# Two attention heads per step instead of one, in the second block of a two-block transformer kernel

## What is computed

```python
def context_attention(q, k, v, sink=None):            # layer 0, context tokens
    s = jnp.einsum('bqhgd,bkhd->bhgqk', q, k)
    _, p = joint_softmax([sink_column(sink, s), s])
    o = jnp.einsum('bhgqk,bkhd->bqhgd', p, v)
...
    # window_attention, layer 0, latent tokens: keys are the context and the band
    _, p_ctx, p_band = joint_softmax([sink_column(sink, s_band), s_ctx, s_band])
...
    # global_attention, layer 1: keys are context and latent, softmax over all
...
    # neighbourhood_attention, layer 1: bias on the latent keys, none on the context
    _ = joint_softmax([s_ctx, s_nb + bias])
```

## Time and profile before

| | |
|---|---|
| median of 3 runs | 2127.74 us (2122.54 to 2133.12) |
| the profiled execution | 2131.4 us, its span 2129.6 us |
| TensorE busy | 1915.3 us, 90% |
| DVE, ACT, POOL busy | 790.7 us, 874.6 us, 940.4 us |
| granted TensorE clock, mean | 0.917 of full speed |

### The profile page before, as it was taken

One profiled execution on the slowest core, in us unless ns is written; L12 is line 12 of the kernel. 1 busy time (PEld: TensorE's weight loads), 2 busy tenths in 40 slices (PEclk: granted clock), 3 DMA queues, 4 the chain that ended last, 5 costly groups with the idle time before them and its releaser, 6 DMA issues.

```text
span 2129.6 us, 26140 instructions
## 1 busy us (share of the span) xinstructions
PE 1915.3 (90%) x10107; PEld 1522.5 (71%) x10107; DVE 790.7 (37%) x1668; ACT 874.6 (41%) x1548; POOL 940.4 (44%) x412
## 2 busy tenths in 40 slices
PE   3999899999779999798879979999998778989997
PEld 2666788777558887697544667888887655669986
DVE  2433332134323321437265444433211663444431
ACT  3543444345444444442334534444321323445652
POOL 2732566766224767343202033444443331035876
PEclk9998899999878999899885989999999887998999
DMA  4422798543127985232100022333222331024653
GB/s 159 159 80 64 239 304 284 217 145 132 60 74 242 303 280 209 84 102 72 60 0 1 1 79 80 99 94 92 92 97 82 91 90 57 1 79 122 187 166 138
DMA packets 248988, 261.91 MB, mean 123 GB/s; under 512 B 13330, under 2 KB 199794, under 8 KB 242594
## 3 DMA queue, kind: packets, MB, share of 16 engines
q1 hardware_dynamic: 247746, 255.62, 37.8%
q10 hardware_dynamic: 1120, 4.63, 0.5%
HBM read 259.18 MB, written 1.05 MB: 122 GB/s over the span
## 4 chain that ended last, share of the span: by engine, by line
PE 79%; DVE 10%; ACT 3%; DMA 3%; issue 2%; SPq 1%; POOL 0%; DVEq 0%; ACTq 0%
PE bank L340 21%; PE bank L341 20%; PE bank L342 19%; PE bank L649 4%; PE bank L672 3%; PE bank L1217 2%; PE bank L657 2%; PE bank L395 1%; PE bank L909 1%; PE bank L935 1%; ACT weights_high L327 1%; PE bank L1561 1%; DVE big L592 1%; DMA weights<-in_ffn_w_down 1%; DVE x_tokens L515 1%
## 5 line engine op out<-in xcount | busy, mean ns | idle before, releaser
L334 POOL TENSOR_TENSOR weights_low<-weights,weights_high 128x1024 fp32r<-128x1024 f32 (+2 forms) x392 | 921.9, 2367 | 1081.8 <-ACT weights_high L327 1081.5
L327 ACT ACTIVATE weights_high<-weights 128x1024 fp32r<-128x1024 f32 (+2 forms) x392 | 400.7, 1036 | 521.7 <-PE bank L342 152.0
L340 PE MATMUL bank<-normed_features_high,weights_high 128*128 128x256 f32 (+1 forms) x1408 | 449.8, 319 | 6.3 <-DVE normed_features_low L424 6.0
L341 PE MATMUL bank<-normed_features_high,weights_low 128*128 128x256 f32 (+1 forms) x1408 | 441.2, 313 | 0.0
L342 PE MATMUL bank<-normed_features_low,weights_high 128*128 128x256 f32 (+1 forms) x1408 | 440.8, 313 | 0.0
L340 PEld LDWEIGHTS bank<-normed_features_high,weights_high 128*128 128x128 f32 x1408 | 272.8, 194 | 65.4 <-issue 36.2
L340 PE MATMUL bank<-weights_high,normed_features_high 128*128 128x512 f32 (+4 forms) x688 | 285.1, 414 | 30.5 <-POOL weights_low L334 17.3
L342 PEld LDWEIGHTS bank<-normed_features_low,weights_high 128*128 128x128 f32 x1408 | 273.5, 194 | 14.1
L341 PEld LDWEIGHTS bank<-normed_features_high,weights_low 128*128 128x128 f32 x1408 | 273.8, 194 | 13.6
L341 PE MATMUL bank<-weights_high,normed_features_low 128*128 128x512 f32 (+4 forms) x688 | 271.9, 395 | 0.0
L342 PE MATMUL bank<-weights_low,normed_features_high 128*128 128x512 f32 (+4 forms) x688 | 270.6, 393 | 0.0
(11 more groups left out here) (240 smaller groups left out, 2246.7 us busy)
## 6 DMA issues: line engine op xcount, KB each, us to landing
work<-in_ada_w SPq DMA_DIRECT2D x48, 1024.0 KB, 7.9
weights<-in_ffn_w_up SPq DMA_DIRECT2D x44, 1024.0 KB, 6.2
weights<-in_ffn_up SPq DMA_DIRECT2D x44, 1024.0 KB, 5.9
weights<-in_ffn_w_down SPq DMA_DIRECT2D x22, 1024.0 KB, 4.9
weights<-in_ffn_down SPq DMA_DIRECT2D x21, 1024.0 KB, 5.0
weights<-in_diff_w_qkv SPq DMA_DIRECT2D x12, 1024.0 KB, 5.0
weights<-in_hyb_w_in SPq DMA_DIRECT2D x10, 1024.0 KB, 5.2
weights<-in_even_w_in SPq DMA_DIRECT2D x8, 1024.0 KB, 5.0
```

The costliest lines, as they stand in the source:

```text
L327: A.eng.activation(high(whigh[:, m % HIGHS, :]), raw(wslot[:, u % SLOTS, :]), ACT.Copy).then_inc(scalar_done, A.one(("A", "high", m)))
L334: G.eng.tensor_tensor(raw(wlow[:, u % SLOTS, :]), raw(wslot[:, u % SLOTS, :]), high(whigh[:, m % HIGHS, :]).bitcast(F32), ALU.subtract).th ...
L340: T.eng.matmul(out_, lh, rh, start=first, stop=False)
L341: T.eng.matmul(out_, ll, rh, start=False, stop=False)
```

## The change

`att_T`, which both phases use, goes through the jobs in twos. In iteration s (0, 2, 4, ...) TensorE issues the scores of s and s+1, piece by piece by turns, then the bias terms of both where there are any; then turn s-2 and turn s-1; then out s-4 and s-3, by turns, 128 keys of the one and 128 of the other. The loops of DVE and ACT keep their order and their constants. Banks: four for scores (0 to 3, by s % 4), two for transposes (4 and 5), two for outputs (6 and 7). Scores now wait for the read of s-4. "2.0 turn2" takes banks 0 to 3 instead of 7, 0, 1 and 2.

```diff
+        SCORE_BANK, TURN_BANK, OUT_BANK = (lambda s: s % 4), (lambda q: 4 + q % 2), (lambda g: 6 + g % 2)
...
-            for s in range(n + OUT):
-                if s < n:
-                    j = jobs[s]
-                    if s >= 3:
-                        e = "V" if jobs[s - 3]["mask"] is not None else "A"
-                        T.eng.wait_ge(SEM[e], done(e, ph, "read", s - 3))
...
-                if 0 <= s - TURN < n:
-                    q = s - TURN
-                    T.eng.wait_ge(vector_done, done("V", ph, "probs", q))
...
-                if 0 <= s - OUT < n:
...
+            for s in range(0, n + OUT, 2):
+                two = [q for q in (s, s + 1) if q < n]
+                for q in two:
+                    if q >= 4:
+                        e = "V" if jobs[q - 4]["mask"] is not None else "A"
+                        T.eng.wait_ge(SEM[e], done(e, ph, "read", q - 4))
+                for x in range(max((len(jobs[q]["scores"]) for q in two), default=0)):
+                    for q in two:
+                        a, b, terms = jobs[q]["scores"][x]
+                        l, r = terms[0]
+                        i = T.eng.matmul(psum[SCORE_BANK(q)][:, a:b], l, r, start=True, stop=(len(terms) == 1))
...
+                for q in two:
+                    a, b, terms = jobs[q]["scores"][-1]
+                    if len(terms) > 1:
...
+                for q in (s - 2, s - 1):
+                    if 0 <= q < n:
+                        T.eng.wait_ge(vector_done, done("V", ph, "probs", q))
+                        if q >= 2:
+                            T.eng.wait_ge(scalar_done, done("A", ph, "turned", q - 2))
+                        for c in range(jobs[q]["n"] // P):
+                            i = T.eng.transpose(psum[TURN_BANK(q)][:, c * P:(c + 1) * P], PB[q % NB][:, c * P:(c + 1) * P], ident)
+                        i.then_inc(tensor_done, T.one(("T", ph, "turn", q)))
+                two = [q for q in (s - 4, s - 3) if 0 <= q < n]
+                for q in two:
+                    j = jobs[q]
+                    T.eng.wait_ge(scalar_done, done("A", ph, "turned", q))
...
+                for c in range(jobs[two[0]]["n"] // P if two else 0):
+                    for q in two:
...
+                        i = T.eng.matmul(psum[OUT_BANK(j["group"])][oa, ob_cols], j["v"][c], PTB[q % NB][:, c * P:(c + 1) * P], start=(first and c == 0), stop=(last and last_c))
...
-              lambda T: (att_T(T, "2.0 attention", js + jl), turns_T(T, "2.0 turn2", turns_m, (7, 0, 1, 2), out_done)),
+              lambda T: (att_T(T, "2.0 attention", js + jl), turns_T(T, "2.0 turn2", turns_m, (0, 1, 2, 3), out_done)),
```

More of the change, by code:

```diff
@@ L636, in program @@
         PTB = [work[:, 2048 + 512 * i:2560 + 512 * i] for i in range(NB)]
+        SCORE_BANK, TURN_BANK, OUT_BANK = (lambda s: s % 4), (lambda q: 4 + q % 2), (lambda g: 6 + g % 2)
         def att_T(T, ph, jobs):
             n = len(jobs)
-            for s in range(n + OUT):
-                if s < n:
-                    j = jobs[s]
-                    if s >= 3:
-                        e = "V" if jobs[s - 3]["mask"] is not None else "A"
-                        T.eng.wait_ge(SEM[e], done(e, ph, "read", s - 3))
[L646 to L650, removed]
-                if 0 <= s - TURN < n:
-                    q = s - TURN
-                    T.eng.wait_ge(vector_done, done("V", ph, "probs", q))
[L654 to L658, removed]
-                if 0 <= s - OUT < n:
-                    q = s - OUT
@@ new lines, in att_T @@
+            for s in range(0, n + OUT, 2):
[9 more added lines that the diff above has]
+                        i = T.eng.matmul(psum[SCORE_BANK(q)][:, a:b], l, r, start=True, stop=(len(terms) == 1))
+                        if x == len(jobs[q]["scores"]) - 1 and len(terms) == 1:
+                            i.then_inc(tensor_done, T.one(("T", ph, "scores", q)))
+                for q in two:
+                    a, b, terms = jobs[q]["scores"][-1]
+                    if len(terms) > 1:
+                        l, r = terms[1]
+                        T.eng.matmul(psum[SCORE_BANK(q)][:, a:b], l, r, start=False, stop=True).then_inc(tensor_done, T.one(("T", ph, "scores", q)))
+                for q in (s - 2, s - 1):
[8 more added lines that the diff above has]
+                for q in two:
@@ L661, in att_T @@
                     j = jobs[q]
                     T.eng.wait_ge(scalar_done, done("A", ph, "turned", q))
-                    ob, oa, ob_cols, first, last, tok = j["out"]
                     if j["open"] and j["group"] >= 2:
@@ L666, in att_T @@
                         T.eng.wait_ge(vector_done, done("V", ph, "group", j["group"] - 2))
[L667 to L673, removed]
+                for c in range(jobs[two[0]]["n"] // P if two else 0):
+                    for q in two:
+                        j = jobs[q]
+                        ob, oa, ob_cols, first, last, tok = j["out"]
+                        last_c = c == j["n"] // P - 1
+                        i = T.eng.matmul(psum[OUT_BANK(j["group"])][oa, ob_cols], j["v"][c], PTB[q % NB][:, c * P:(c + 1) * P], start=(first and c == 0), stop=(last and last_c))
+                        if last_c:
+                            i.then_inc(tensor_done, T.one(("T", ph, "out", q)))
         def att_V(V, ph, jobs, aside={}):
@@ L688, in att_V @@
                     if j["mask"] is not None:
-                        V.eng.tensor_tensor_reduce(out=PB[s % NB][:, 0:j["n"]], in0=psum[s % 3][:, 0:j["n"]], in1=j["mask"],
+                        V.eng.tensor_tensor_reduce(out=PB[s % NB][:, 0:j["n"]], in0=psum[SCORE_BANK(s)][:, 0:j["n"]], in1=j["mask"],
                                                           scale=1.0, scalar=(3e38 if init is None else init), op0=ALU.add, op1=ALU.min,
@@ L692, in att_V @@
                     else:
-                        V.eng.tensor_reduce(mn, psum[s % 3][:, 0:j["n"]], AX_X, ALU.min).then_inc(vector_done, V.one())
+                        V.eng.tensor_reduce(mn, psum[SCORE_BANK(s)][:, 0:j["n"]], AX_X, ALU.min).then_inc(vector_done, V.one())
                         if init is not None:
@@ L719, in att_V @@
                         V.eng.wait_ge(scalar_done, done("A", ph, "group", j["group"]))
[L720 removed]
+                        V.eng.tensor_tensor(low, psum[OUT_BANK(j["group"])][:, src_cols], high.bitcast(F32), ALU.subtract).then_inc(vector_done, V.one(("V", ph, "group", j["group"])))
         def att_A(A, ph, jobs, aside={}):
@@ L731, in att_A @@
                         A.eng.wait_ge(vector_done, done("V", ph, "probs", s - NB))
-                    src = PB[s % NB] if j["mask"] is not None else psum[s % 3]
+                    src = PB[s % NB] if j["mask"] is not None else psum[SCORE_BANK(s)]
                     mn = mxs[:, s % NB:s % NB + 1]
@@ L744, in att_A @@
                     m = jobs[q]["n"]
-                    A.eng.activation(PTB[q % NB][:, 0:m], psum[3 + q % 2][:, 0:m], ACT.Copy).then_inc(scalar_done, A.one(("A", ph, "turned", q)))
+                    A.eng.activation(PTB[q % NB][:, 0:m], psum[TURN_BANK(q)][:, 0:m], ACT.Copy).then_inc(scalar_done, A.one(("A", ph, "turned", q)))
                 if 0 <= s - CLOSE < n and jobs[s - CLOSE]["close"] is not None:
@@ L749, in att_A @@
                     A.eng.wait_ge(tensor_done, done("T", ph, "out", q))
-                    A.eng.activation(dst, psum[5 + jobs[q]["group"] % 2][:, src_cols], ACT.Copy).then_inc(scalar_done, A.one(("A", ph, "group", jobs[q]["group"])))
+                    A.eng.activation(dst, psum[OUT_BANK(jobs[q]["group"])][:, src_cols], ACT.Copy).then_inc(scalar_done, A.one(("A", ph, "group", jobs[q]["group"])))
         def weave(dense, steps, plan):
```

4 lines of the change are left out of this document (2 added, 2 removed).

## The result

The changed kernel is slower: 2146.72 us in the median of four runs (2141.71 to 2149.39) against 2126.64 us for the kernel before in the same comparison (2122.54 to 2133.12). The ratio is 1.0089, with a 95% interval from 1.0056 to 1.0122. The forecast was slower, at 2160 us. The profiled execution of the changed kernel took 2141.71 us, the shortest of its four, so its trace shows 10 us of the 20: its span is 2139.9 us against 2129.6.

The account below looks back on a forecast made before the run. TensorE was taken to bound the attention stages. The slow-clock sum of +53 us, less 20 for one third of the way back, gave +33 on 2131.4: 2164, or 2160 against the median; range 2130 to 2190.

Parts of the forecast that it names:

- The bound before: In the two attention stages TensorE is almost alone in the chain; a windowed job costs its 2.66 us at 2.4 GHz.
- the packing's price: Per pair: scores as one job, values as one plus 0.05 us, transposes as two; TensorE's work 5.32 to 3.3 us.
- Rival 4: Values: column groups do not overlap with 64-column loads between them; about +50 us on top, 2210; chance 0.08.
- The ring: In each pair DVE's two steps and TensorE's second transpose, values and next scores add up: windowed 6.10 us against 5.32.
- Rival 2: Attention stages: TensorE stays the bound, 3.3 us a windowed pair, about -60 us, 2068, chance 0.02; smaller gain, 2112, 0.03.
- one third of the way back from all-slow: Both attention stages: bursts mostly at 1.2 GHz; the slow-clock sum of +53 us less 20 gives +33.
- forecast ends of 42.7 and 58.7: First stage, seven windowed cycles from scores 16: 42.7 us with the fast clock, 58.7 with the slow one.
- rival 3: Both stages: the clock behaves about as before, rising for good some 20 us into the long jobs; +5 us, 2132; chance 0.15.
- the likeliest case: Attention stages: the ring as forecast with bursts mostly at 1.2 GHz; 2148 to 2182 us; chance 0.62.
- the signs named: Trace after: scores and values paired, TensorE waiting for DVE's probs, its busy share 55 to 75%, clock mostly 0.5 to 0.7.
- the 6 us: Windowed pairs: the prediction is wrong if such a pair takes under 6 us.
- The last one: Long jobs of both stages: the prediction is wrong if the clock rests at 1.00 there.

Follow-up runs that it names:

- probs_and_copy_first: The changed kernel with DVE doing probs of s-2 before the read of s, and ACT copying transposes of s-3 before exp of s: 2085.77 us, ratio 0.9802.
- values_in_sequence: The changed kernel with all value products of a pair's first job before those of the second: 2155.92 us, ratio 1.0125 against the kernel before.
- turns_two_later: The changed kernel with transposes of s-4 and s-3, values of s-6 and s-5, group copies two steps later: 2061.24 us, ratio 0.9699 against the kernel before.
- gaps_filled: The changed kernel with five identity products before each transpose of jobs 6 to 29, changing no result: 2128.66 us, ratio 1.0010 against the kernel before.

## Why the prediction was right, and where it was off

**The bound before, and the packing's price: right.** A pair's scores cost one job and its values one job and nothing more (1.09 with its end, the same as eight passes, not 0.05 over). Rival 4, that column groups would not overlap with 64-column loads between them, is out: 16 passes in 1.09 us.

**The ring: right, in place, releaser and size.** The windowed pair at full clock is 6.17 us from scores at 1177.30 to 1183.47 in the chain (6.10 forecast on average; this is one with L730, for which the terms give 6.31, and the pair of 7.18 us is 5.83 without the slow clock, where they give 5.89), a near pair 5.96 or 6.30 by turns, 6.13 on average (6.20). The context part to scores 16 ends 45.5 us into the stage, against 47 forecast and 40 before. probs_and_copy_first takes one DVE step out of the sum and values_in_sequence lengthens one term, and the pair follows within 0.03 us. Rival 2, TensorE still the bound, is nearly what turns_two_later shows (66 us under the kernel before, 60 forecast), with DVE almost as full: its mechanism is real and it needed the distance that the change took away.

**The clock: the step that was off.** I took one third of the way back from all-slow, +33 us, and the profiled execution has +11 in the two stages (11.5 and -0.1). From scores 16 to scores 30 of the first stage the seven windowed pairs took 49.4 us between the forecast ends of 42.7 and 58.7: 58% of the way back. The six global ones took 43.4 between 33.4 and 47.1: 27%. The seven near ones took 42.9 where the fast end was 43.4: all of it. The sentence that fails is "I expect a fall in or behind nearly every such stretch", and so does its sequel, that the clock returns near the burst's end and is "lost in the next idle stretch". In the global pairs it is the other way round, as the next paragraph shows. In the near pairs TensorE is busy 73% of the time (31.37 of 42.9 us), its idle pieces are 0.96 and 0.55 or 0.88 us, and the clock stayed at 1.00. In the windowed pairs it is busy 63%, mostly with pieces of 1.64 and 0.8 to 1.1, and the mean is 0.78; in the global ones the pieces are 1.37 and 0.5 to 0.9, and it is 0.70. I had priced both alike, although the bias products of the second near job fill the time ahead of the first transpose. The busy share as measured does not tell them apart: it is 73% in the global pairs too (31.76 of 43.4 us), because their work runs slowly. At full clock it would be 3.3 of 5.56 us, 59%, an estimate from the prediction's terms. That less idle time brings the clock back is shown by gaps_filled and, without added work, by probs_and_copy_first. The length of the pieces alone does not decide: in values_in_sequence one near pair with pieces of 0.96 and 0.88 us did fall (its values take 2.78 us, in the others 1.58).

**The rule on idle gaps.** By the section on HAM oscillation in "TensorE: Matmul & The Clock Gate" (the Trainium skill), taken alone, gaps as short as these should keep the clock. The trace does not agree: in the global pairs from scores 4 to scores 16 no idle piece was longer than 1.38 us, and the mean clock there was 0.70. One of these pairs:

```profile
1813.23 2.08 PE L653 MATMUL bank<-qk_features 64*128 64x512 f32 x4
1816.68 0.66 PE L667 MATMUL bank<-con,work 128*128 128x128 f32 x4 [1.37 <-DVE work L720]
1817.87 0.65 PE L667 MATMUL bank<-con,work 128*128 128x128 f32 x4 [0.54 <-DVE work L720]
1818.46 1.85 PE L681 MATMUL bank<-work,big 128*64 128x128 f32 x16
1820.23 2.01 PE L653 MATMUL bank<-qk_features 64*128 64x512 f32 x4
```

The transposes beside the idle pieces run at full speed, and the values and the next scores, which stand back to back, run slowly. By stretch, the clock was 1.00 from 1815.5 to 1818.5, with TensorE busy 1.28 of 3.0 us, and 0.55 from 1818.5 to 1822.3, with TensorE busy 3.74 of 3.8. So in such a pair the clock fell behind the emptier stretch, in the burst, and was back for the next emptier one, where it is of least use. The measurement decides: here short gaps, close together, went with a clock that fell and came back in every pair. What decides between these pairs and the near ones is not shown.

**Where the number lies.** The forecast was 32 us slower and the median is 20 us slower. 2146.72 lies inside the range of 2130 to 2190, but just under the 2148 to 2182 that was the likeliest case's own, and above rival 3's 2132: the global pairs are the likeliest case, the near pairs are rival 3, and the windowed ones are half of each. The mechanism was right; that the total stayed in the range owes something to this mixture. Of the signs named, the releaser (L720, the old L710), the pairing, the 6 us and TensorE's share (56% to 73%) came as said. The last one did not: for the near jobs, 43 us of the second stage, the clock did rest at 1.00. The 1 us named for a cold start behind each stage is not in the 2164 either; that changes nothing.

**The rest.** The execution that was profiled shows 10 us of the median's 20. The other three executions took 2145.0 to 2149.4 us; no trace tells where in them the 3 to 8 us more lie.

## What to carry to other kernels

When two steps of a software pipeline are merged into one, ask for each wait how many iterations back its releaser now lies: here one transpose came to wait for work on scores issued in its own iteration, and two engines that had overlapped took turns, which cost more than twofold packing gained. Draw the ring (who waits for whom within one iteration), add its terms from the rows, and compare it with the busiest engine. If the ring is longer, lengthen the distance or move what is not needed out of it; with the same matmuls the distance alone took the kernel from 0.9% slower to 3.0% faster.

## What the runs showed of the hardware

- Jobs on the two row halves overlap even where they are issued one after the other (three jobs of 256 keys in 1.13 us in the earlier trace rows); for the column halves the order by turns matters: 16 passes 1.09 us by turns, 1.58 in sequence (at 1.2 GHz 1.98 and 2.88). It did not matter for the 8 passes of a context pair at 1.2 GHz (1.12 and 1.13 us).
- Two idle pieces of 1.37 and 0.5 to 0.9 us in each pair of some 7 us went with a mean granted clock of 0.70; of 0.96 and 0.55 to 0.88 us, in 6 us, with 1.00 in the changed kernel, and with one fall in seven pairs in values_in_sequence. In a global pair the low clock lay in the unbroken work behind the idle pieces and not in them. Filling them with products that nobody reads brought it back to 1.00 and paid for itself (2128.66 against 2146.72 us), though it cost 0.5 us in each near pair, which had the full clock already.
- With the scores paired alone the clock was at 1.00 from 1158 us on, through the windowed jobs; before, the first five of them ran at 0.50.
